# Memory attention in the recurrent layers: score products from high and low halves, and where the halves are made

## The reference

```
def mem_cross_attention(h, mem_n, wq, wkv, wo):
    q = (h @ wq).reshape(B, T, XA_HEADS, XA_HEAD_DIM)
    kv = (mem_n @ wkv).reshape(B, M, 2, XA_HEADS, XA_HEAD_DIM)
    k, v = kv[:, :, 0], kv[:, :, 1]
    s = jnp.einsum('bthd,bmhd->bhtm', q, k).astype(jnp.float32) * (XA_HEAD_DIM ** -0.5)
    p = jax.nn.softmax(s, axis=-1).astype(h.dtype)
    o = jnp.einsum('bhtm,bmhd->bthd', p, v).reshape(B, T, D_MODEL)
    return o @ wo
```

## Time and profile before

| | us |
|---|---|
| median of 3 runs | 3250.34 |
| profiled execution | 3248.06 |
| its span, first to last instruction | 3246.3 |
| TensorE busy | 3213.2 |
| VectorE busy | 1698.0 |
| ScalarE busy | 1166.0 |
| attention over the memory, layer 0, from 1680.48 | 75.95 |

### The profile page before, as it was taken

The page is one execution under the profiler, slowest core; times in us unless marked ns, Lnnn a source line. Parts: engine busy times, 40 slices in busy tenths (PEclk is TensorE's granted clock), DMA queues, the critical chain, the costliest instruction groups (busy, mean ns, idle before and its releaser), DMA issues.

```text
span 3246.3 us, 39625 instructions
## 1 busy us (share of the span) xinstructions
PE 3213.2 (99%) x14786; PEld 2634.1 (81%) x14786; DVE 1698.0 (52%) x2490; ACT 1166.0 (36%) x1847; POOL 0.2 (0%) x4
## 2 busy tenths in 40 slices
PE   9999999999999999999999999999999999999998
PEld 7777778788888888888887888888888888788887
DVE  6564445564544554346655554345443675465443
ACT  5663555532222322233533322232222344332222
POOL 0000000000000000000000000000000000000000
PEclk9999999999999999999999999999999999999999
DMA  4333333232222222232321222222223223132222
GB/s 145 102 94 98 95 100 104 84 118 94 96 95 97 97 97 97 98 110 75 117 85 65 94 95 96 97 98 97 97 97 113 86 90 112 46 101 95 96 97 91
DMA packets 90696, 313.32 MB, mean 97 GB/s; under 512 B 10192, under 2 KB 12624, under 8 KB 90192
## 3 DMA queue, kind: packets, MB, share of 16 engines
q1 hardware_dynamic: 83376, 294.69, 27.2%
q10 hardware_dynamic: 7200, 16.97, 1.7%
HBM read 309.52 MB, written 2.10 MB: 96 GB/s over the span
## 4 chain that ended last, share of the span: by engine, by line
PE 96%; DVE 2%; ACT 1%; issue 1%; DMA 0%; DVEq 0%; ACTq 0%
PE ps L1087 30%; PE ps L1089 29%; PE ps L1088 29%; PE ps L1274 1%; PE ps L1358 1%; PE ps L1263 1%; PE ps L1163 1%; PE ps L1252 1%; PE ps L1306 0%; PE ps L1289 0%; PE ps L1371 0%; PE ps L1255 0%; PE ps L1310 0%; PE ps L1395 0%; PE ps L1300 0%
## 5 line engine op out<-in xcount | busy, mean ns | idle before, releaser
L1087 PE MATMUL ps<-x_hi,whi 128*128 128x512 f32 x2400 | 945.0, 394 | 0.0
L1089 PE MATMUL ps<-x_hi,wlo 128*128 128x512 f32 x2400 | 934.7, 389 | 0.0
L1088 PE MATMUL ps<-x_lo,whi 128*128 128x512 f32 x2400 | 934.0, 389 | 0.0
L1412 ACT ACTIVATE whi<-raw 128x1024 fp32r<-128x1024 f32 (+1 forms) x555 | 583.2, 1053 | 897.4 <-DMA raw<-in_weights 895.1
L1699 DVE TENSOR_TENSOR wlo<-raw,whi 128x1024 fp32r<-128x1024 f32 x553 | 675.3, 1223 | 429.9 <-ACT whi L1412 421.1
L1087 PEld LDWEIGHTS ps<-x_hi,whi 128*128 128x128 f32 x2400 | 450.7, 188 | 97.6 <-issue 3.9
L1089 PEld LDWEIGHTS ps<-x_hi,wlo 128*128 128x128 f32 x2400 | 450.5, 188 | 94.5
L1088 PEld LDWEIGHTS ps<-x_lo,whi 128*128 128x128 f32 x2400 | 450.8, 188 | 94.0 <-issue 2.4
L1087 PE MATMUL ps<-h_hi,whi 128*128 128x512 f32 (+1 forms) x902 | 346.4, 384 | 0.0
L1089 PE MATMUL ps<-h_hi,wlo 128*128 128x512 f32 (+1 forms) x902 | 346.2, 384 | 0.0
L1088 PE MATMUL ps<-h_lo,whi 128*128 128x512 f32 (+1 forms) x902 | 346.2, 384 | 0.0
(11 more groups left out here) (290 smaller groups left out, 3312.4 us busy)
## 6 DMA issues: line engine op xcount, KB each, us to landing
raw<-in_weights SPq DMA_DIRECT2D x553, 512.0 KB, 3.2
bias<-in_biasB ACTq DMA_DIRECT2D x16, 384.0 KB, 3.2
bias<-in_biasA ACTq DMA_DIRECT2D x16, 256.0 KB, 3.1
mem_raw<-in_mem ACTq DMA_DIRECT2D x3, 1024.0 KB, 7.0
x_res<-in_x SPq DMA_DIRECT2D x8, 256.0 KB, 6.2
x_res<-in_x ACTq DMA_DIRECT2D x8, 256.0 KB, 3.3
out_x<-x_res SPq DMA_DIRECT2D x16, 128.0 KB, 1.9
raw<-in_weights SPq DMA_DIRECT2D x2, 256.0 KB, 4.2
```

Of the source, the lines that this page charges most:

```text
L1087: pe.matmul(out, hi, xhi, start=start, stop=False)
L1088: pe.matmul(out, hi, xlo, start=False, stop=False)
L1089: return pe.matmul(out, lo, xhi, start=False, stop=stop)
L1412: return act.activation(out, in_, ACT.Copy, scale=scale)
```

## The change

The two score products in float32 become six in fp32r, from halves of queries and keys. The low halves are written in place of XQ and XK; the high halves lie where the pooling branch, the memory's halves, the mixer's output halves and the feed-forward gate had their places. Each chunk's halves come from a `split` step, and the list of steps says where: keys 0 to 3 behind the first four output columns of the mixer, queries 0, keys 4 and 5 behind job 1, queries 1, keys 6 and 7 behind job 2, queries 2 to 7 behind the next turn. The score tile waits for the low halves of its head's second chunks.

```diff
-    def attend(tiles, work, after_pv=None, places=None):
+    def attend(tiles, work, after_pv=None, places=None, behind=()):
...
-        s.behind_turn = []
+        s.behind_turn = list(behind)
...
+        def split_row(name, c, need):
+            step("split", id=(name, l, c), src=(name, c), dst=(name, c), need=need)
+
         for m in range(DC):
             j = begun[m][1]() if m < 3 else column("w_out_2", l, m, rows=mix_rows, **mixed(m))
             step("refresh", n=norm, m=m, gain=f"xa_norm_2_{l}", need=("evac", j))
+            if m < 4:
+                split_row("XK", m, [("evac", jk[m])])
+        mixed_out = ("evac", j)
...
-                column("xa_wq_2", l, c, rhs="x", n=T, evac="scale", dst=("XQ", c), need=needx)
-                jq[c] = s.njobs - 1
+                jq[c] = column("xa_wq_2", l, c, rhs="x", n=T, evac="scale", dst=("XQ", c), need=needx)
                 needx = {}
+                if s.behind_turn is not None:
+                    s.behind_turn.append(lambda: split_row("XQ", c, [("evac", jq[c])]))
             queries.append(go)
-        for go in queries[:3]:
-            go()
+        queries[0]()
+        queries[1]()
+        split_row("XQ", 0, [("evac", jq[0])])
+        split_row("XK", 4, [mixed_out])
+        split_row("XK", 5, [mixed_out])
+        queries[2]()
+        split_row("XQ", 1, [("evac", jq[1])])
+        split_row("XK", 6, [mixed_out])
+        split_row("XK", 7, [mixed_out])
...
-        attend([dict(kind="X", h=h, t=t, l=l, need=[("evac", jk[2 * h + 1])], queries=(jq, 2 * h + 1),
+        attend([dict(kind="X", h=h, t=t, l=l, need=[("olo", ("XK", l, 2 * h + 1)), ("olo", ("XQ", l, 2 * h + 1))],
...
+               behind=[lambda: split_row("XQ", 2, [("evac", jq[2])])])
...
+        XQL, XKL = area("x_q_lo", 8, [P, DC, T], F32R), area("x_k_lo", 0, [P, DC, NM], F32R)
+        XQH = area("x_q_hi", 94, [P, DC, T], F32R)
+        XKH = [area(f"x_k_hi_{kb}", kb, [P, 2, NM], F32R) for kb in (110, 112, 68, 92)]
...
-                        if what == "X":
-                            jq, c = a["queries"]
-                            pe.wait_ge(*on("evac", jq[c]))
...
-                            mm = pe.matmul(sc, XQ[:, 2 * h + c, tt], XK[:, 2 * h + c, :],
-                                           start=(c == 0), stop=(c == 1))
+                            qh, ql = halves(("XQ", 2 * h + c))
+                            mm = three(sc, qh[:, tt], ql[:, tt], *halves(("XK", 2 * h + c)), c == 0, c == 1)
...
-                    copy(MIXH[:, a["dst"][1], :], buf(a["src"])).then_inc(*sig("ohi", a["id"]))
+                    copy(halves(a["dst"])[0], buf(a["src"])).then_inc(*sig("ohi", a["id"]))
...
-                    c = a["dst"][1]
+                    hi, lo = halves(a["dst"])
                     after_own()
                     dve.wait_ge(*on("ohi", a["id"]))
-                    dve.tensor_tensor(MIXL[:, c, :], buf(a["src"]), MIXH[:, c, :].bitcast(F32), ALU.subtract)\
-                        .then_inc(*sig("olo", a["id"]))
+                    dve.tensor_tensor(lo, buf(a["src"]), hi.bitcast(F32), ALU.subtract).then_inc(*sig("olo", a["id"]))
```

More of the change, by code:

```diff
@@ L737, in build_schedule @@
         begun = [s.column_parts("xa_wo_2", l, m, tuple(range(DC)), 6, **attended(m)) for m in range(3)]
-        attend([dict(kind="X", h=h, t=t, l=l, need=[("evac", jk[2 * h + 1])], queries=(jq, 2 * h + 1),
+        attend([dict(kind="X", h=h, t=t, l=l, need=[("olo", ("XK", l, 2 * h + 1)), ("olo", ("XQ", l, 2 * h + 1))],
                      need_v=[("xev", (x_group[2 * h], NM // P - 1))]) for h in range(NHEAD) for t in range(NT)],
-               queries[3:] + [start for start, _ in begun], places=(3, 7, 11, 15, 20, 28, 30, 32))
+               queries[3:] + [start for start, _ in begun], places=(3, 7, 11, 15, 20, 28, 30, 32),
+               behind=[lambda: split_row("XQ", 2, [("evac", jq[2])])])
         norm += 1
@@ L927, in buf, with halves @@
             return bufs[where[0]][:, where[1], :]
+        def halves(where):
+            name, c = where
+            if name == "XK":
+                return XKH[c // 2][:, c % 2, :], XKL[:, c, :]
+            hi, lo = {"MIX": (MIXH, MIXL), "XQ": (XQH, XQL)}[name]
+            return hi[:, c, :], lo[:, c, :]
         def col(name, m=0):
```

## The result

The changed kernel takes 3264.84 us (median of 6 runs, 3264.11 to 3266.42) against 3250.19 for the kernel before beside it (6 runs, 3248.43 to 3251.32): ratio 1.0046, 95% interval 1.0034 to 1.0059, slower. Forecast were 3265.3 and slower. The profiled execution took 3265.03 us around a span of 3263.2.

A forecast was written before the change was run, and what follows sets the result against it. TensorE, busy 99% of the span, was taken to bound the kernel. Terms summed to 6.6 us a layer, 13.2 for two, plus 1.7 for a clock fall: +14.9 on 3250.34, forecast 3265.3 us, range 3256 to 3272.

The forecast's parts named there:

- (a): Head 0: tile 0 waits for the subtraction of queries 1, listed behind evacuation 2; +1.61 us a layer.
- (b): Head 1: tile 4 waits for copies and subtractions of queries 2 and 3, listed behind the turned tile 0; +1.57 us.
- (c): Tiles 5 and 6, between jobs, wait for nothing and save 0.29 us; tile 15 likewise 0.15.
- (d): Head 2: tile 8 waits for the subtraction of queries 5, behind high half and turned tile on ScalarE; +0.51 us.
- (e): Behind head 1's last turn: the subtraction of queries 6 stands ahead of tile 9's maximum, delaying the values' product; +1.04 us.
- (f): Head 3: tile 12 waits for the halves of queries 7, and the following chain delays the values' product; +2.33 us.
- The one fall: One clock fall of full price behind an added wait, most likely at tile 12: +1.7 us; none to eight possible.
- Standing still: Added TensorE waits at the score line, released by VectorE's query halves: 1.8, 1.6, 0.6 and 2.8 us in each layer.
- the pitch of 0.12: Six fp32r score products of 256 columns at 0.12 us each: 0.72 us a tile against 0.87.
- The rival that the clock falls at most of the waits: Six falls of 1.7 us in place of one, over both layers' attentions: 3273.7 us; chance 0.11.
- rival (A): The products win and the halves hide: the saving alone, 4.7 us, giving 3245.6; chance 0.06.
- All else as it was: Sign in the profile: attention stretches longer by 6.6 us, everything outside them unchanged.

The follow-up runs named there:

- products alone: Kernel before with three fp32r products in place of each fp32 one, low parts left out and no halves made: 3245.49 us, ratio 0.9991.
- queries 1 alone: Changed kernel with the halves of queries 1 listed ahead of query job 2 instead of behind its evacuation: 3265.67 us, ratio 1.0048.
- job 7: Changed kernel with query job 7 at place 19 instead of 20, ahead of head 1's values: 3255.2 us, ratio 1.0017.
- the place 2: Kernel with all query jobs and halves moved one job ahead, with query job 4 at place 2 instead of 3: 3246.29 us, ratio 0.9990.
- the moved halves: Changed kernel with query jobs one place earlier, halves ahead of the next job and the attention's first output column moved: 3246.97 us, again 3247.2.
- the even queries later: Changed kernel with halves of queries 2, 4 and 6 moved from behind the next turn to just ahead of the next query job: 3261.29 us, ratio 1.0037.
- float32 products: Changed kernel with halves and waits kept, but score products done once each in float32 from the high halves: 3267.46 us, ratio 1.0056.
- queries 1 and both keys moved up: Changed kernel with the halves of queries 1 and of keys 6 and 7 all ahead of query job 2: 3264.39 us, ratio 1.0043.

## Why the prediction was right

The steps, each beside what the timelines before and after give, layer 0 / layer 1:

- (a) head 0: +1.61 said, +1.54 / +1.54 measured.
- (b) head 1, tile 4: +1.57; +1.55 / +1.53.
- (c) tiles 5 and 6: -0.29; -0.31 / -0.31. Tile 15: -0.15; -0.17 / -0.16.
- (d) head 2, tile 8: +0.51; +0.48 / +0.51.
- (e) head 1's values: +1.04; +1.09 / +1.10.
- (f) head 3 to head 2's values: +2.33; +3.56 / +2.43. In layer 0 it holds the clock's fall, which costs 1.1.
- Sum 6.6; 7.74 / 6.64. The one fall was to cost 1.7 and to come at tile 12; it came there and cost 1.1. Behind the tile TensorE waits 0.43 and 0.37 us in layer 1 and 0.71 in one wait in layer 0; that is 0.1 less, so it isn't shown where the rest of the 1.7 went.
- Standing still of 1.8, 1.6, 0.6 and 2.8 was forecast, 1.62, 1.63, 0.41 and 2.80 measured.

These steps held because VectorE and ScalarE took their instructions in the order of the list, and each link had a row of the trace (the score tile at 1690.63 stands in rows 5, not in rows 4 as the prediction has it). The halves' prices (0.40 taken for the key pair's two, 0.40 and 0.42 measured; 0.63 and 0.69 for the queries') and the pitch of 0.12 were right too. The output columns of the mixer did not wait, as the earlier trace rows said, and the experiments took (a), (e) and (f) away and cut (b), each by nothing but the place of halves or of a query job. The rival that the clock falls at most of the waits came half true in two other kernels, not in this one.

Smaller errors. The saving of 4.7 us of rival (A) is not to be had: products alone gave 3.4 in the stretches. The prediction's sum did not need it, as it counted only tiles that nothing holds up, (c) among them. The total was met more closely than the sum deserves. "All else as it was" failed in the mixer of layer 1: the clock's fall there, which is that of the earlier trace rows and in the kernel before cost nothing, now costs 1.5, and the prediction had counted falls in the attentions alone. By the profiled executions the time grew by 17.0 us, not 14.9: 0.5 less in the attentions than forecast, 2.5 more outside them. That the median lies within 0.5 us of the forecast is luck: the profiled execution before was 2.1 us under its median of six, the one after 0.2 over. Three of my later expectations missed. For queries 1 alone I had not listed what else stood between evacuation 2 and tile 0's maximum, the very reading that the prediction asks for; for job 7 I had 2.9 for 3.8 us; and the place 2 was to gain 0.66 and gave 0.24.

**The mixer of layer 1.** It takes 963.6 us before (end of one stretch to the start of the next), 965.1 after and 966.4 with the moved halves. It is not the work of the key halves: with the same halves in it, it takes 963.7 to 963.8 in the kernels with queries 1 ahead, with the even queries later and with job 7 earlier. It is the clock. TensorE waits there twice for `h_qt`, 6.7 us apart. Before, the clock falls behind the first of these waits, the products between the two run longer, and the second wait is shorter by as much. After, it falls behind the second wait, with nothing behind that to hide it. The second wait before, both waits after, and the second wait with the even queries later:

```profile
2657.28 1.13 PE L1358 MATMUL ps<-h_qt,h_q 128*128 128x128 f32 x8 [1.18 <-DVE h_qt L2056]
```

```profile
2659.20 1.15 PE L1382 MATMUL ps<-h_qt,h_q 128*128 128x128 f32 x8 [1.89 <-DVE h_qt L2079]
...
2665.91 2.05 PE L1382 MATMUL ps<-h_qt,h_q 128*128 128x128 f32 x8 [2.81 <-DVE h_qt L2079]
```

```profile
2664.03 1.13 PE L1383 MATMUL ps<-h_qt,h_q 128*128 128x128 f32 x8 [2.81 <-DVE h_qt L2080]
```

With the even queries later the clock is 1.00 all through this mixer, as it is with the products alone; in both kernels TensorE waits 4.7 us in all for `h_qt` (3.1 before), and the mixer takes 963.7 and 963.6. So a second wait of 2.81 is what stands there with no fall at all, and a fall between the two waits costs nothing. Over all the profiled executions: no fall or one behind the first wait, 963.6 to 963.8; one behind the second, 964.8 to 965.2; with the moved halves, where the granted clock is 0.66 over ten microseconds behind the second wait in place of 0.83, 966.4. Why the fall comes behind the one or the other is open.

## To carry to other kernels

When helper operations are added on engines that are half idle, count not their busy time but the place in each engine's in-order list: between the producer and the awaiting product stand all operations listed ahead, and a pair needs one job's lead. A version with the lead costs no more than the bare products; without it, the change loses four times what it can gain. A wait of about two microseconds or more can also be followed by a fall of the clock. One fall cost 1.1 to 1.7 us here, 2.8 where the granted clock was 0.66 over ten microseconds, and nothing where a wait behind it took up the loss. Taking one wait away can bring the fall at another.

## What the runs showed that I had not expected

The clock's fall does not follow the length of the wait alone. A wait of 1.97 us ahead of the same value products kept the granted clock at 1.00 in the changed kernel, and was followed by a fall (0.83 over ten microseconds) in the two kernels in which nothing but the start of the attention had changed, in both layers, at 1.69 us each. A wait of 2.80 at tile 12 was followed by the fall in layer 0 and not in layer 1; with float32 products, and with queries 1 alone ahead, the other way round; with the even queries later, in both. A wait of 2.81 for `h_qt` was followed by it in the changed kernel and not with the even queries later. The Trainium skill (TensorE: Matmul & The Clock Gate, What's actually happening) ties the fall to idle time of the array; the trace agrees in that every fall in an attention stood behind a wait of TensorE, of 1.97 us or more. That a wait of the same length does and does not bring it is what these runs show. What decides between them wasn't found. So a kernel can be improved at one place and be no faster: queries 1 and both keys moved up won 1.85 us a layer and gave 1.69 back.
